# Three edits to the schedule of a two-layer decoder trunk: the last FFN tile, GpSimd's first loads, the first norm

## The reference

```python
h = rms_norm(h_res, norm_mix[l])
u = h @ w_in[l]
y_a = mla_mixer(...); y_b = nsa_mixer(...); y_c = rglru_mixer(...); y_d = ssd_mixer(...)
y = concatenate([rms_norm(y_a), rms_norm(y_b), rms_norm(y_c), y_d])
h_res = h_res + y @ w_out[l]
h = rms_norm(h_res, norm_ffn[l])
if l % 2 == 0: f = swiglu(h, w_gate, w_up, w_down)        # (silu(h@wg) * (h@wu)) @ wd, inner width 3584
else:          f = moe_ffn(h, router, ...)                # top 2 of 8 experts, each a swiglu of the same size
h_res = h_res + f
```

## Time and profile before

| | |
|---|---|
| median of 3 runs | 1654.93 us (1654.78 to 1655.82) |
| the profiled execution: its own time / its span | 1653.88 / 1652.3 us |
| TensorE busy (weight loads) | 1545.6 us, 94% (1292.2 us, 78%) |
| VectorE, ScalarE, GpSimd busy | 76%, 61%, 4% |
| mean granted clock of TensorE | 0.947 |
| HBM read, mean rate | 436.03 MB, 269 GB/s |
| chain that ended last | PE 90%, DVE 5%, issue 2%, ACT 2%, DMA 1% |

### The profile page before, as it was taken

The page is one execution under the profiler, slowest core; times in us unless marked ns, Lnnn a source line. Parts: engine busy times, 40 slices in busy tenths (PEclk is TensorE's granted clock), DMA queues, the critical chain, the costliest instruction groups (busy, mean ns, idle before and its releaser), DMA issues.

```text
span 1652.3 us, 20337 instructions
## 1 busy us (share of the span) xinstructions
PE 1545.6 (94%) x7454; PEld 1292.2 (78%) x7454; DVE 1254.6 (76%) x1281; ACT 1014.7 (61%) x918; POOL 73.9 (4%) x106
## 2 busy tenths in 40 slices
PE   6988899999798975999999999999999999999996
PEld 4977688888697964887887887887887887887884
DVE  6776654444558566988988988988988988988985
ACT  5455444434355443777777777777777777777763
POOL 3001000000000011000000000000000000000000
PEclk9977999999898786999999999999999999999998
DMA  9600655556350033999998999998998998999990
GB/s 276 242 1 17 197 182 188 194 178 191 108 183 26 2 110 110 388 394 335 395 396 307 395 396 324 393 397 308 393 396 308 393 395 309 393 396 325 393 396 31
DMA packets 189878, 444.67 MB, mean 269 GB/s; under 512 B 9633, under 2 KB 15918, under 8 KB 189822
## 3 DMA queue, kind: packets, MB, share of 16 engines
q1 hardware_dynamic: 185214, 427.82, 70.6%
q0 software_dynamic: 4608, 16.10, 3.8%
HBM read 436.03 MB, written 7.86 MB: 269 GB/s over the span
## 4 chain that ended last, share of the span: by engine, by line
PE 90%; DVE 5%; issue 2%; ACT 2%; DMA 1%; POOL 0%; DVEq 0%; ACTq 0%; POOLq 0%
PE bank L407 25%; PE bank L408 25%; PE bank L406 24%; PE bank L534 2%; PE bank L666 2%; PE bank L461 2%; PE bank L632 2%; PE bank L537 1%; ACT w_hi L1199 1%; PE bank L647 1%; DVE w_lo L1584 1%; PE bank L676 1%; PE bank L853 0%; PE bank L386 0%; DVE hT L1539 0%
## 5 line engine op out<-in xcount | busy, mean ns | idle before, releaser
L1584 DVE TENSOR_TENSOR w_lo<-ring,w_hi 128x2048 fp32r<-128x2048 f32 x375 | 854.0, 2291 | 215.2 <-ACT w_hi L1199 214.4
L1199 ACT ACTIVATE w_hi<-ring 128x2048 fp32r<-128x2048 f32 x375 | 717.0, 1916 | 249.3 <-PE bank L406 249.2
L407 PE MATMUL bank<-w_hi,xT_hi 128*128 128x512 f32 x896 | 354.5, 396 | 5.8 <-ACT w_hi L1199 5.8
L408 PE MATMUL bank<-w_hi,xT_lo 128*128 128x512 f32 x896 | 350.4, 391 | 0.0
L406 PE MATMUL bank<-w_lo,xT_hi 128*128 128x512 f32 x896 | 240.3, 390 | 0.0
L407 PE MATMUL bank<-w_hi,hidT_hi 128*128 128x512 f32 x560 | 223.9, 400 | 16.0 <-DVE hidT_lo L1591 16.0
L408 PE MATMUL bank<-w_hi,hidT_lo 128*128 128x512 f32 x560 | 221.4, 395 | 0.0
L407 PEld LDWEIGHTS bank<-w_hi,xT_hi 128*128 128x128 f32 x896 | 168.8, 188 | 40.1 <-ACT w_hi L1199 6.2
L406 PEld LDWEIGHTS bank<-w_lo,xT_hi 128*128 128x128 f32 x896 | 168.7, 188 | 35.7
L408 PEld LDWEIGHTS bank<-w_hi,xT_lo 128*128 128x128 f32 x896 | 169.0, 189 | 33.9
L407 PE MATMUL bank<-w_hi,hT_hi 128*128 128x512 f32 (+2 forms) x384 | 151.5, 398 | 11.1 <-DVE hT_lo L1544 9.9
(11 more groups left out here) (332 smaller groups left out, 1378.0 us busy)
## 6 DMA issues: line engine op xcount, KB each, us to landing
ring<-in_moe_w_gate_dram SPq DMA_DIRECT2D x112, 1024.0 KB, 8.0
ring<-in_moe_w_up_dram SPq DMA_DIRECT2D x112, 1024.0 KB, 8.4
ring<-in_moe_w_down_dram SPq DMA_DIRECT2D x112, 1024.0 KB, 8.0
ring<-in_ffn_w_gate_dram SPq DMA_DIRECT2D x14, 1024.0 KB, 5.1
ring<-in_ffn_w_up_dram SPq DMA_DIRECT2D x14, 1024.0 KB, 5.2
ring<-in_ffn_w_down_dram SPq DMA_DIRECT2D x14, 1024.0 KB, 4.9
ring<-in_w_in_dram SPq DMA_DIRECT2D x12, 1024.0 KB, 5.2
ring<-in_w_out_dram SPq DMA_DIRECT2D x8, 1024.0 KB, 7.8
```

The source lines that it names most:

```text
L407: pe.matmul(o, x_hi, w, start=start, stop=False)
L408: return pe.matmul(o, x_lo, w, start=False, stop=False)
L1199: act.activation(w_hi[:, (base + at) % SPLIT, :], ring[:, i, :], ACT.Copy).then_inc(hi_ready, 1)
L1584: dve.tensor_tensor(w_lo[:, v, :], ring[:, (base + at) % RING, :], w_hi[:, v, :].bitcast(F32), ALU.subtract).then_inc(lo_ready, 1)
```

## The change

On ScalarE and VectorE alike, `turned(NCH - 1)` moves up between the splits of the last chunk's two down units. At the start: ScalarE scales x into `hn` for the first norm, right behind its squares; VectorE computes the lam and the rope arguments after its split of unit 1; GpSimd issues the SSD vectors and `lru_w` first, waits for the low part of unit 5 (`lo_ready` 6), and then issues the mixer weights, the router and `gfin`. The last two get a semaphore of their own.

```diff
+        late_in = sem("late_in")
-        N_MISC = 3 + 2 + 2
+        N_MISC = 3 + 2
@@ TensorE, ahead of the router's product
-            pe.wait_ge(misc_in, 16 * N_MISC)
+            pe.wait_ge(late_in, 16 * 2)
@@ GpSimd
                 roots(1, 1)
                 if l == 0:
-                    mixer_weights(0)
                     for i, src in enumerate((ssd_dt_bias, ssd_a_log, ssd_d)):
                         pool.dma_start(ssd_par[:, :, i, :], src[:, :].partition_broadcast(P)).then_inc(misc_in, 16)
...
+
+                    pool.wait_ge(lo_ready, 6)
+                    mixer_weights(0)
                     pool.dma_start(router[:, :, :], moe_router[0].rearrange("(k p) e -> p k e", p=P))\
-                        .then_inc(misc_in, 16)
-                    pool.dma_start(gfin[:, :], norm_final[:].partition_broadcast(P)).then_inc(misc_in, 16)
+                        .then_inc(late_in, 16)
+                    pool.dma_start(gfin[:, :], norm_final[:].partition_broadcast(P)).then_inc(late_in, 16)
@@ ScalarE, end of ffn
                 split(at_down(NCH - 1, 0))
+                turned(NCH - 1)
                 split(at_down(NCH - 1, 1))
-                turned(NCH - 1)
@@ ScalarE, layer 0, behind the squares
                 if l == 0:
+                    for tb in range(TB):
+                        act.wait_ge(rstd_ready, tb + 1)
+                        act.activation(hn[:, tb, :], xres[:, tb, :], ACT.Copy, scale=rstd[:, tb:tb + 1])\
+                            .then_inc(hn_ready, 1)
                     split(p)
                     split_input(0)
@@ VectorE: the same lines, now inside two functions
-            dve.wait_ge(inv_ready, ROPE // 2)
-            dve.wait_ge(pos_in, 16)
-            link(dve.tensor_copy(pos_f[:, :], pos_i[:, :]))
...
+            def rope_start():
...
             b = filled()
             link(dve.tensor_copy(par[:, :, :], b[:, 0:2 * P].rearrange("p (l c) -> p l c", l=L)))
             take_bank(dve.tensor_copy(pe_t[:, :, :], b[:, 2 * P:2 * P + L * CLEN].rearrange("p (l c) -> p l c", l=L)))
...
+            def lam_start():
...
-            dve.wait_ge(x_in, 16 * TB)
             def normed(l2, turn_set):
-                for tb in range(TB):
+                for tb in range(TB if l2 else 0):
@@ VectorE, layer 0
                 split(p + 1)
+                if l == 0:
+                    lam_start()
+                    rope_start()
                 split(p + 2, UB + SSD_H)
```

More of the change, by code:

```diff
@@ L1471, in signal @@
             def signal(ins, name, s):
-                counts[name] = counts.get(name, 0) + 1
+                counts[name] = counts.get(name, TB if name == "hn" else 0) + 1
                 ins.then_inc(s, 1)
@@ L1511, in _ @@
-            link(dve.tensor_scalar(rr[:, 1, :, :], rr[:, 1, :, :], np.pi / 2, None, ALU.add))
-            signal(dve.tensor_scalar(rr[:, :, :, :], rr[:, :, :, :], -3.1415925, 3.1415925, ALU.max, ALU.min),
-                   "rope", rope_args)
+            def rope_start():
+                dve.wait_ge(inv_ready, ROPE // 2)
+                dve.wait_ge(pos_in, 16)
+                link(dve.tensor_copy(pos_f[:, :], pos_i[:, :]))
+                for tb in range(TB):
+                    link(dve.tensor_scalar(ang[:, tb, :], inv[:, :], pos_f[:, tb:tb + 1], None, ALU.mult))
+                TURN = 2 * np.pi
+                MAGIC = 1.5 * 2.0 ** 23
+                PARTS = [6.28125, 1.93500518798828125e-3]
+                PARTS.append(TURN - sum(PARTS))
+                for i in range(2):
+                    link(dve.tensor_scalar(rk[:, i, :, :], ang[:, :, :], 1 / TURN, 0.25 * i, ALU.mult, ALU.add))
+                    link(dve.tensor_scalar(rk[:, i, :, :], rk[:, i, :, :], MAGIC, None, ALU.add))
+                    link(dve.tensor_scalar(rk[:, i, :, :], rk[:, i, :, :], -MAGIC, None, ALU.add))
+                    src = ang
+                    for part in PARTS:
+                        s_ = src[:, :, :] if src is ang else rr[:, i, :, :]
+                        link(dve.scalar_tensor_tensor(out=rr[:, i, :, :], in0=rk[:, i, :, :], scalar=-part, in1=s_,
+                                                      op0=ALU.mult, op1=ALU.add))
+                        src = rr
+                link(dve.tensor_scalar(rr[:, 1, :, :], rr[:, 1, :, :], np.pi / 2, None, ALU.add))
+                signal(dve.tensor_scalar(rr[:, :, :, :], rr[:, :, :, :], -3.1415925, 3.1415925, ALU.max, ALU.min),
+                       "rope", rope_args)
@@ L1518, in _ @@
             take_bank(dve.tensor_copy(pe_t[:, :, :], b[:, 2 * P:2 * P + L * CLEN].rearrange("p (l c) -> p l c", l=L)))
[L1519 to L1523, removed]
-            dve.wait_ge(x_in, 16 * TB)
+            def lam_start():
+                lam = par[:, :, PR["lam"]:PR["lam"] + 2]
+                link(dve.tensor_scalar(lru_t[:, :, 5, :], lam, -1.0, None, ALU.mult))
+                signal(dve.tensor_tensor(lru_t[:, :, 0, :], lru_t[:, :, 5, :], lam, ALU.min), "lam", lam_args)
+                signal(dve.tensor_scalar(half_b[:, :, :], par[:, :, PR["lbg"]:PR["lbg"] + 4], 0.5, None, ALU.mult),
+                       "half_b", half_b_ready)
             def normed(l2, turn_set):
-                for tb in range(TB):
+                for tb in range(TB if l2 else 0):
                     dve.wait_ge(rstd_ready, 7 * (l2 // 2) + 5 * (l2 % 2) + tb + 1)
```

## The result

The changed kernel takes 1628.35 us (median of 4 runs, 1627.69 to 1630.06), beside 1655.38 us for the kernel before (1654.78 to 1659.7, 4 runs on the same chip). The ratio is 0.9833, 95% interval 0.982 to 0.9847: 27 us are gone. The forecast was 1634.8 with a range of 1631 to 1640, so the sign and the places were right and the size was 6.5 us too small. The profiled execution took 1628.72 us by itself, span 1627.0 against 1652.3: 25.3 us of span.

The account below looks back on a forecast made before the run. TensorE, busy 94% of the span, was taken to bound the kernel, with time to gain only where it waits. 15.8 (pass ends) + 0 (dense pass) + 4.3 (start) = 20.1 us faster gave 1634.8 us, range 1631 to 1640.

Parts of the forecast that it names:

- The last tile of a pass: End of each expert pass: TensorE's wait for `hidT_lo` goes, 1.98 us each, 15.8 us over eight passes.
- up to 3 us: Allowance in the range's low end for phases in which the clock rises sooner after an idle spell.
- The row quoted for the clock: Profile row of one 122.87 us expert pass, TensorE busy 119.96 us, clock 1.00; cited against a lower clock.
- What is late next: Behind the moved tile: unit 41's split stays covered, ScalarE's idle 2.32 us pays for the 1.98, whole gain kept.
- The dense pass: End of the dense pass: TensorE's 1.6 us wait for the turned tiles stays; saving taken as 0.
- The start: Kernel start: TensorE's transposes of `hn` begin at about 10.05 instead of 14.32, 4.3 us, passed on to the end.
- The sum: Whole kernel: 15.8 + 0 + 4.3 = 20.1 us faster, forecast 1634.8 us.
- Loads bind: Rival: loads bind the expert passes at 373 GB/s, only the start's gain is left, 1650.6; chance 0.06, in part or whole.
- the rule that was weighed: Expert passes: HBM side binds loads at about 358 GB/s per core, so the first edit would bring nothing; trace disagreed.
- Start given back: Rival: late unit 2 load and unit 3 split leave 0 to 1 us of the start's gain, 1638.5; chance 0.12.
- Slower by the clock: Rival: TensorE without rest in expert passes gets a lower clock, say 0.95, 1683; chance 0.04 with other no-faster mechanisms.

Follow-up runs that it names:

- the start alone: The changed kernel with the `turned(NCH - 1)` moves undone on both engines, so only the start differs from the kernel before: 1651.09 us, ratio 0.9982.
- the run with the loads early: The changed kernel with GpSimd's loads at the start back in the old order, mixer weights first without the wait: 1632.52 us, ratio 0.9851.
- ScalarE's move alone: The kernel before with `turned(NCH - 1)` moved up between the two splits on ScalarE only, VectorE's order as before: 1667.77 us, ratio 1.009.

## Why the prediction was too small

**The last tile of a pass: mechanism right, size wrong.** This is the step that failed, the term "1.98 us. Eight passes give 15.8". The tile is early, the wait is gone, nothing behind it is late. But it brought 8 x 2.1 + 4 x 1.6 = 23.2 us. Of the 7.4 us missing, 6.4 are the clock, and 1.0 is that the shift is 2.1 and not 1.98 per pass. I worked the whole term from one pass end, at 762 to 773 us, and that was one of the four where the clock stayed up. The next end, 122 us on, showed a product of 0.63 us behind the same wait. The bound had the same flaw: its low end in time allowed "up to 3 us" for the clock, without a row. It lay in the periods of the passes all along: four of 123.3 beside 121.7. The row quoted for the clock holds the pass behind an end where the clock stayed up. It stops at 889.30, 0.4 us behind the next wait, just where the first slow spell begins.

**What is late next: right.** ScalarE's result of the previous expert waited 0.7 us once between 740 and 1600 us, instead of 6.2 us in 7 pieces, so ScalarE's pauses did pay for the shift. No wait for `w_hi` or `hid` appeared in the first chunks. The period forecast was 120.9 and came out at 119.6. Part of that is my cut: the stretch of 122.87 us does not begin and end at the same point of two passes. The true period there is 121.7, and 1.98 less would have been 119.7.

**The dense pass: right.** 1.6 us of waiting before and after.

**The start: right, by its trace.** 4.6 us for the transposes and 4.5 for the first product, where I took 4.3; the second `hn` and the rest were covered. Unit 2 landed at 21.6, inside 19 to 25. The rope work was done in time for ScalarE's sine at 26.4, and unit 3 was split by 31.5, before the 34.6 that was allowed. The mixer's loads were issued at 39.8 to 44.7, GpSimd's `rstd` step came at 45.35, and line 565's products waited for no DMA. The lam instructions took 0.17 us each, at the low end. How much of it reaches the end of the kernel is less sure: 4.1 us with the start alone, with an interval of 0.2 to 6.

**The tail: missing.** I carried the gain to the end unchanged. There 2.3 us are lost: 1.0 in a longer idle spell ahead of the combine, and 1.3 in the combine, at a lower clock. It has the other sign and made the total error smaller. The part at the lower clock is of the same kind as the slow spells in the passes; why the idle spell grew is not shown.

**The sum** was 20.1; the measured parts are 23.2 + 4.4 - 2.3 = 25.3 in the profile, and 27 between the medians. The remaining 1.7 us lie within the spread of the runs.

**The rivals.** *Loads bind:* no. TensorE and ScalarE waited for no load in the passes, and the two passes shown ran at 376 and 377 GB/s, above the 373 of before. For the rule that was weighed, the 358 GB/s of the Trainium skill (page "DMA: Bandwidth & Descriptors", section "Where 436 GB/s comes from"), that is one more measurement against it on this core. *Start given back:* no, but the run with the loads early shows that it was a real danger: 2.1 us of it come back if GpSimd's loads stay in front. *Slower by the clock:* wrong sign. With TensorE working without a rest the clock did not fall (1.00 in both passes shown); in the passes it fell only behind a rest. Apart from the "up to 3 us" in the low end, I had given the clock a role only in the case against the change, and that is why its gain was missed.

**What stays open.** Which pass ends are hit: the same four in the kernel before and in the one with only the start changed, but not the ones after ScalarE's move alone, and the length of the wait does not tell them apart. Why the pause ahead of the combine is as long as it is. And what makes the time up to the first expert pass differ between kernels whose code there is the same, and between two profiles of one kernel (662.9 and 668.6 us for the changed one). In these profiles the spread of the totals comes from there. The clock in the mixers differs too (0.70 to 0.83 between 480 and 640 us), but nothing here shows that this is the cause.

## What to carry to other kernels

Price a wait of TensorE at its length plus what the products behind it lose, and read those behind every occurrence of the wait, not behind one: compare periods and the granted clock of the few microseconds after each. Where a short wait can't be removed, small products into a free bank can keep the clock up, if they stand exactly where TensorE would idle. That worked where the idle time was a wait for another engine, and not ahead of the combine, where it stood at the engine's own register load and branches. Count too on a gain at one place being given back in part at the next pause. When two engines hand a tile on, test each one's order alone: here one of them brought nearly all of it, and the other by itself made it slower. And where totals vary by several us, compare the part of the profile that repeats.

## What the runs showed of the hardware

- An idle spell of 1.8 us in a stream of products that was otherwise without a pause was followed by 1.2 GHz in four of eight cases, at 1.6 us each; one of 2.7 us in three of eight, two of which made their periods 1.6 and 2.9 us longer. With 0.24 us of idling left it was none of eight.
- Products queued on TensorE ahead of a register load and branches did not hide them: the idle spell was 3.54 us without and 4.40 us with 2.84 us of products in front. One branch instead of three turns of the loop, with the load early, left 1.42, and that was a wait for ScalarE. The three turns and the late load left only 1.39, also a wait for ScalarE, where TensorE had waited 2.7 us at the pass end before.
- The eight products of the combine took 3.70 us after idle spells of 1.39 and 1.42 us (clock 1.00), 5.39 after 2.3 to 2.6, 5.11 after 3.38, and 6.5 to 6.7 after 3.5 and more.
- VectorE's smallest instructions took 0.17 us in the changed kernel at 22 us, where GpSimd issued no DMA. In the kernel before, at the start, two of the same three took 0.76 and 0.86 us beside GpSimd's issue of `w_cmp` (10.72 to 12.95), and the one between them 0.16. That the issue is the cause is not shown:

```profile
11.10 0.76 DVE L1520 TENSOR_SCALAR lru_t<-par 128x4 f32<-128x4 f32 x1
11.89 0.16 DVE L1521 TENSOR_TENSOR lru_t<-lru_t,par 128x4 f32<-128x4 f32 x1
12.09 0.86 DVE L1522 TENSOR_SCALAR half_b<-par 128x8 f32<-128x8 f32 x1
```

- Unit 2's load landed 8.4 us earlier when 2.15 MB of GpSimd's loads no longer ran beside it (29.98 and 21.57), and at 29.30 again when they did.
